# Three transfers of 112, 8 and 8 rows in place of one of 128, for the gate weights of four experts

## What is computed

```
hid = silu(xs @ w_gate[e]) * (xs @ w_up[e])      # w_gate, w_up: 1024 x 512
out = hid @ w_down[e]                            # w_down: 512 x 1024
```

## Time and profile before

| what | value |
|---|---|
| median of 3 runs | 1076.56 us (1076.35 to 1080.98) |
| the profiled execution, its own time | 1078.08 us |
| its span, from the first to the last instruction | 1076.3 us |
| PE busy | 915.3 us (85%) |
| VectorE busy | 540.1 us (50%) |
| read from memory (HBM) | 312.24 MB |
| last expert weights landed | 1062.10 us |

### The profile page before, as it was taken

One profiled execution on the slowest core, in us unless ns is written; L12 is line 12 of the kernel. 1 busy time (PEld: TensorE's weight loads), 2 busy tenths in 40 slices (PEclk: granted clock), 3 DMA queues, 4 the chain that ended last, 5 costly groups with the idle time before them and its releaser, 6 DMA issues.

```text
span 1076.3 us, 19223 instructions
## 1 busy us (share of the span) xinstructions
PE 915.3 (85%) x8378; PEld 703.6 (65%) x8378; DVE 540.1 (50%) x1008; ACT 347.4 (32%) x684; POOL 76.2 (7%) x113
## 2 busy tenths in 40 slices
PE   9999999999999999999999997766666666657665
PEld 8587788489999888988989954433333333334432
DVE  2476588858888767888767642211112111212121
ACT  4411355246776526455553331000001000000001
POOL 3101810000000000330010000000000000000000
PEclk9999999999999999999999999988889787889888
DMA  9344463685454664975446999999999999999994
GB/s 347 108 172 170 147 236 101 223 287 173 157 185 160 221 233 162 289 244 189 160 150 253 428 382 421 429 427 430 429 429 427 429 427 431 428 429 431 426 430 173
DMA packets 76106, 316.71 MB, mean 294 GB/s; under 512 B 3999, under 2 KB 27840, under 8 KB 63472
## 3 DMA queue, kind: packets, MB, share of 16 engines
q1 hardware_dynamic: 71252, 302.24, 71.3%
q0 software_dynamic: 4624, 13.14, 4.0%
q10 hardware_dynamic: 140, 0.04, 0.0%
HBM read 312.24 MB, written 1.06 MB: 291 GB/s over the span
## 4 chain that ended last, share of the span: by engine, by line
PE 59%; DMA 27%; DVE 8%; ACT 4%; issue 2%; ACTq 0%; SPq 0%; POOL 0%; DVEq 0%
PE ps L461 57%; DMA w<-in_w_up 19%; DMA w<-in_w_gate 6%; DMA w<-in_w_down 2%; DVE sp L1860 1%; DMA rot<-q 1%; PE ps L587 0%; PE ps L2702 0%; DVE acc L923 0%; ACT sp L1851 0%; ACT hts L2809 0%; ACT sd L2183 0%; PE ps L2115 0%; ACTq L3041 0%; DVE w L961 0%
## 5 line engine op out<-in xcount | busy, mean ns | idle before, releaser
L461 PE MATMUL ps<-w,xg 128*32 128x256 f32 x2048 | 158.9, 474 | 107.4 <-DMA w<-in_w_up 83.8
L461 PE MATMUL ps<-hb,sp 128*128 128x256 f32 x1824 | 224.5, 283 | 0.0
L461 PEld LDWEIGHTS ps<-hb,sp 128*128 128x128 f32 x1824 | 218.6, 188 | 3.9 <-issue 3.0
L461 PEld LDWEIGHTS ps<-w,xg 128*32 128x32 f32 x2048 | 84.4, 132 | 180.3 <-issue 156.3
L1860 DVE TENSOR_TENSOR sp<-w,sp 128x1024 fp32r<-128x1024 f32 x122 | 144.4, 1220 | 37.1 <-ACT sp L1851 37.1
L1851 ACT ACTIVATE sp<-w 128x1024 fp32r<-128x1024 f32 x122 | 122.1, 1051 | 42.1 <-PE ps L461 40.5
L2876 DVE TENSOR_TENSOR cst<-ps,cst 64x256 f32<-64x256 f32 x31 | 13.3, 428 | 224.0 <-ACT cst L2796 224.0
L2796 ACT ACTIVATE cst<-ps 64x256 f32<-64x256 f32 x31 | 11.7, 377 | 324.9 <-PE ps L461 324.9
L2902 DVE TENSOR_TENSOR ost<-ps,cst 32x256 f32<-32x256 f32 x120 | 50.5, 420 | 100.2 <-PE ps L461 97.4
L461 PE MATMUL ps<-w,hts 128*32 128x256 f32 x1024 | 62.1, 382 | 13.2 <-ACT hts L2809 11.4
L461 PE MATMUL ps<-sp,ab 128*128 128x512 f32 x264 | 61.7, 395 | 0.0
(11 more groups left out here) (415 smaller groups left out, 1164.4 us busy)
## 6 DMA issues: line engine op xcount, KB each, us to landing
w<-in_w_down SPq DMA_DIRECT2D x36, 2048.0 KB, 35.1
w<-in_w_gate SPq DMA_DIRECT2D x32, 2048.0 KB, 28.6
w<-in_w_up SPq DMA_DIRECT2D x32, 2048.0 KB, 32.4
w<-in_w_in SPq DMA_DIRECT2D x13, 2048.0 KB, 9.6
w<-in_w_up SPq DMA_DIRECT2D x22, 1024.0 KB, 7.7
w<-in_w_ada SPq DMA_DIRECT2D x8, 2048.0 KB, 8.5
w<-in_w_out SPq DMA_DIRECT2D x4, 2048.0 KB, 9.0
w<-in_w_ada POOLq DMA_DIRECT2D x8, 768.0 KB, 5.3
```

The lines of the kernel that those rows point to most:

```text
L461: return q.eng.matmul(o, l, r, start=start, stop=stop, skip_group_check=True)
```

## The change

```
+        EIGHTS = (6, 13, 20, 27)
+
+        def in_eights(e):
+            rows16 = A["w_gate_2"][0, e, :, :].rearrange("(p k) n -> p (k n)", p=128)
+            return [(lambda sl, a=a, b=b: sl[a:b, :], rows16[a:b, :]) for a, b in ((0, 112), (112, 120), (120, 128))]
         for n, (e_, z) in enumerate(order):
-            place(("ex", e_, z), EXS[n % 10], expert_parts(e_)[z])
+            place(("ex", e_, z), EXS[n % 10], *(in_eights(e_) if z == 0 and e_ in EIGHTS else [expert_parts(e_)[z]]))
```

## The result

| | before | after |
|---|---|---|
| median of 6 runs | 1079.66 us (1076.35 to 1082.25) | **1120.3 us** (1119.24 to 1127.75) |
| ratio to before, 95% interval | | **1.039** [1.0369, 1.041] |
| the profiled execution, its own time | 1078.08 us | 1127.75 us |
| its span | 1076.3 us | 1126.0 us |
| last expert weights landed | 1062.10 us | 1112.3 us |

The change costs **40.6 us** by the medians, where I had forecast 16.9. The ratio isn't formed from the two medians: 3.9% of 1080 us is 42 us.

A forecast was written before the change was run, and what follows sets the result against it. The expert stage was taken as bound by its DMA transfers; 13.7 for narrow rows + 5.7 for the 112 rows - 2.5 slack = +16.9 us, against 1076.56 a forecast of 1093.5 us (+1.6%), range 1074 to 1106 us.

The forecast's parts named there:

- What bounds the kernel: Expert stage: bound by its DMA transfers, so a later landing of the last weights delays the end one for one.
- Issue and completions: SyncE's 8 more transfers and the 32 or so more completions per place: costed at nothing.
- The sign and the place: Slower, with GB/s dips near 680, 790, 890 and 990 us, DMA share near 1, and a tail of 10 us or more.
- The 112 rows: The 112-row transfer at each of four gate matrices: from nothing to +11.4 us in all, middle taken, +5.7 us.
- The price of the rate: Transfers to few partitions: 258 GB/s, read from 32-row transfers in the earlier trace, used as the upper bound for the 112 rows.
- Narrow rows, +13.7 us: The two 8-row transfers per place: 2.0 us a row on the same eight engines, +3.4 us a place, +13.7 us in all.
- The slack, -2.5 us: Tail of the transfers: eight engines finish some 5 us early and may absorb loss; half taken, -2.5 us.
- D: Narrow writers also hold up engines writing those partitions for other matrices: +29.3 us, 1105.9 us; counted with the forecast, together 0.64.
- A: Narrow rows run at full pace and the late eight engines are relieved: 1074.4 us, chance 0.22.
- B: Narrow rows run at full pace but the loaded eight engines are the late ones: +2.4 us, 1079.0 us, chance 0.09.
- C: Rows of the small transfers are spread so no engine gets more: nothing changes, 1076.6 us, chance 0.03.

The follow-up runs named there:

- experiments 1 and 9: Against the kernel before, gate matrices cut into three column ranges of all 128 rows: ratio 1.0005; cut into four transfers of every fourth row: ratio 1.0013.
- expert 6 alone: Only the gate matrix of expert 6, the first place, split as in the change, the others as in the kernel before: 1086.39 us, ratio 1.0053.
- experiment 3: The change with one transfer of 16 rows in place of the two of 8, the 112 rows kept: 1111.87 us, ratio 1.0289 to the kernel before.
- experiment 12: Every-fourth-row split of the four gate matrices, its last transfer cut into four of 8 rows: 1095.22 against 1081.75 us for the kernel before, ratio 1.0125.
- experiments 4 and 5: Rows 32 to 127 in one transfer, rows 0 to 31 in four of 8 rows: spread four apart 1118.46 us, neighbouring blocks 1128.95 us.

## Why the prediction was wrong

**What bounds the kernel** was right. The delays of the four places add up to the end without loss, and the last 16 matmuls start with the landing, [1.08 <-DMA w<-in_w_down].

**Issue and completions at nothing** was right: experiments 1 and 9 have as many transfers as the change or more, and cost nothing.

**The sign and the place** were right: dips at 680 us and at the three other places with the share near 1, and a longer tail.

**The 112 rows are the step that failed, and with them the neighbours in the queue.** I costed the 112 rows at 0 to 2.8 us a place and took 1.4. The packets of expert 6 alone give 3.6 us, above my upper bound, and those of experiment 3's first dip 3.1. What the transfers do to other matrices I put at nothing: beside the 112 rows I let only the eight engines with narrow rows lose, and only on these rows. In fact the matrix behind loses another 2.9 us at expert 6, over all 16 engines. Experiment 3, with 112 and 16 rows and no 8-row transfer, costs 31 us, 8 a place, where I had 1.4 for the 112 rows. The price of the rate was about right for the start of a dip: I took 258 GB/s from the earlier trace rows, and the first dip begins at 246 and 257. But over its 15 us it averages 214. And I let only the 1.84 MB of the transfer itself go slowly, 7.1 us in place of 4.3. For lack of a row I then took the middle of a range whose upper bound was too low.

Why 112 rows cost is shown less far. The Trainium skill (DMA: Bandwidth & Descriptors, The descriptor swizzle) gives each engine of a 128-partition transfer exactly one port: four rows and the four rows 32 above. Then no two engines meet at a port. My explanation is that a transfer whose shape gives the engines other rows breaks this, for its own rows and, since the engines are microseconds apart, for the neighbours of the queue whose engines are still or already at those ports. The runs agree with it as far as they go: 429 GB/s is kept with 128 rows, with 64 at step 2 and with 32 at step 4, all shapes that can give every engine rows of its own port; it is lost with 112 rows, although these reach all 16 ports. Which rows an engine gets is seen in no run, only how many. The same page (Back-pressure in remote DMA) says of transfers between cores that a saturated port also holds up its engine's other traffic; there are none here, and no run shows this separately. A rival is untested: since the rows read and the partitions written always changed together, the engines could also be in each other's way where they read. A run that reads its rows from other places in memory and writes the same partitions would tell.

**Narrow rows, +13.7 us**: mis-sized less, and for an incomplete reason. At expert 6 alone a narrow row takes 1.6 us, where I had 2.0. Two 8-row transfers in place of one of 16 rows add 9 to 11 us (experiment 3 against the change), and an 8-row transfer costs 0.84 us where its rows are spread (experiment 12). Neighbouring rows cost 0.66 us more than spread ones (experiments 4 and 5). These are below my +1.7 us for each. That both small transfers go to the same eight engines was right.

**The slack, -2.5 us**: nothing shows it. For the first place alone the slice lacks 7.2 us and the time grows by 5.7 (7.3 by the medians), which leaves room for at most some 1.5 us. The loaded eight are neither the early nor the late ones: at the end of that run they finish between 1065.1 and 1071.0, the others between 1064.5 and 1070.6.

**The places are not alike.** I multiplied one price by four. The dips grow from 7.5 to 13.3 us in the changed kernel, and the first and last place alone cost 5.7 and 9.5 us. Even with all places at the last one's price alone, four would be 38 us. The engines drift apart even in the kernel before: they end a matrix within 2.5 us of each other at 675 us, and the last one within 7.1 us. So late in the stage more transfers are under way at once, and more of them can be slowed. That fits the growth, but it was not tried by itself: its cause is open.

**Rivals.** D, that the narrow writers hold up others, came nearest: others are held up. But it had this for the 8-row transfers alone, and ended at +29.3 us. (Its terms as written, 4 x (2 x 2.5 - 0.61) + 11.4, give 29.0; the rest is rounding.) A, B and C fall with the first dip. My range ended at D because I had bounded each term by the transfer's own bytes.

## What to carry to other kernels

In a weight stream at full rate (429 GB/s here) it matters which rows each transfer has. Before cutting a transfer by rows, ask which rows each piece reaches. Cut by columns, or by every second or fourth row, the rate stayed; cut by blocks of rows, a 4.9 us matrix cost 8 us more, with its neighbours in the queue. When a dip's rate is taken from a row, its length must be bounded too, by the whole time in which such a transfer is on any engine.

## What the runs showed that I had not expected

- Two halves of 64 rows each cost 33 us over four matrices if they are rows 0 to 63 and 64 to 127, and nothing (ratio 0.9992) if they are the even and the odd rows.
- With 32-row transfers of every fourth row the rate stays at the full 431 GB/s; with 16-row ones of every eighth row it is 183.
- The slowed stretch is three times as long as the matrix takes normally (15 against 4.9 us).
- The same split costs more later in the stage, by the slices: alone, and the more so after others.
- More packets are slow (190 in the first dip, 334 in the last) than the split matrix has rows (128).
